# A mixture of experts as one unbroken sequence of steps: the next expert's first up product between the last transposes and the last down product

## What is computed

```python
def moe_swiglu(h, w_router, w1, w3, w2):
    logits = (h @ w_router).astype(jnp.float32)
    top_val, top_idx = lax.top_k(logits, TOP_K)          # TOP_K = 2 of N_EXPERTS = 8
    probs = jax.nn.softmax(top_val, axis=-1)
    combine = jnp.sum(jax.nn.one_hot(top_idx, N_EXPERTS, dtype=jnp.float32) * probs[..., None], axis=-2)
    out = jnp.zeros_like(h)
    for e in range(N_EXPERTS):
        out = out + combine[..., e:e + 1] * swiglu(h, w1[e], w3[e], w2[e])   # (silu(h @ w1) * (h @ w3)) @ w2
    return out
```

## Time and profile before

| | us |
|---|---|
| median of 3 runs | 2117.86 |
| lowest, highest | 2117.47, 2119.53 |
| time of the profiled execution | 2120.26 |
| its span, first to last instruction | 2118.5 |
| busy in the span: PE | 2027.8 |
| DVE | 1609.6 |
| ACT | 1233.7 |

### The profile page before, as it was taken

One profiled execution on the slowest core, in us unless ns is written; L12 is line 12 of the kernel. 1 busy time (PEld: TensorE's weight loads), 2 busy tenths in 40 slices (PEclk: granted clock), 3 DMA queues, 4 the chain that ended last, 5 costly groups with the idle time before them and its releaser, 6 DMA issues.

```text
span 2118.5 us, 28922 instructions
## 1 busy us (share of the span) xinstructions
PE 2027.8 (96%) x10759; PEld 1728.0 (82%) x10759; DVE 1609.6 (76%) x1256; ACT 1233.7 (58%) x1013; POOL 16.5 (1%) x22
## 2 busy tenths in 40 slices
PE   7999999989997999999979999999999999999997
PEld 6998888879997988888868878888887888888885
DVE  5878865755445878955766888898888889888985
ACT  4544455444433554455446777777777777777774
POOL 0000000000000000000000000000000000000000
PEclk9999999999999999999988999999999999999999
DMA  8523455245554522455247999999999999999994
GB/s 279 160 80 100 140 178 179 89 151 188 179 190 136 177 82 90 145 164 186 91 149 260 387 344 378 359 362 368 353 379 341 382 358 364 375 341 372 351 375 179
DMA packets 240481, 516.97 MB, mean 244 GB/s; under 512 B 11519, under 2 KB 34167, under 8 KB 240412
## 3 DMA queue, kind: packets, MB, share of 16 engines
q1 hardware_dynamic: 238124, 507.60, 68.1%
q0 software_dynamic: 2288, 8.41, 1.1%
HBM read 513.86 MB, written 2.12 MB: 244 GB/s over the span
## 4 chain that ended last, share of the span: by engine, by line
PE 87%; DVE 7%; ACT 3%; issue 2%; DMA 0%; SPq 0%; DVEq 0%; ACTq 0%
PE PS L476 25%; PE PS L478 25%; PE PS L477 25%; PE PS L547 7%; DVE lo L1533 2%; ACT hi L1102 2%; PE PS L1002 1%; PE PS L978 1%; PE PS L496 1%; PE PS L758 0%; DVE a_act L1634 0%; DMA rows<-in_knorm_c 0%; PE PS L948 0%; PE PS L789 0%; DVE t_n L1556 0%
## 5 line engine op out<-in xcount | busy, mean ns | idle before, releaser
L1533 DVE TENSOR_TENSOR lo<-raw,hi 128x2048 fp32r<-128x2048 f32 x481 | 1095.0, 2290 | 295.0 <-ACT hi L1102 292.3
L1102 ACT ACTIVATE hi<-raw 128x2048 fp32r<-128x2048 f32 x481 | 919.6, 1915 | 337.8 <-PE PS L478 330.5
L476 PE MATMUL PS<-hi,e_hi 128*128 128x512 f32 x896 | 355.3, 397 | 1.4 <-DVE e_lo L1556 1.4
L478 PE MATMUL PS<-hi,e_lo 128*128 128x512 f32 x896 | 350.2, 391 | 0.0
L477 PE MATMUL PS<-lo,e_hi 128*128 128x512 f32 x896 | 350.2, 391 | 0.0
L476 PE MATMUL PS<-hi,actT_hi 128*128 128x512 f32 x640 | 253.9, 397 | 4.6 <-DVE lo L1533 4.1
L478 PE MATMUL PS<-hi,actT_lo 128*128 128x512 f32 x640 | 249.6, 390 | 0.0
L477 PE MATMUL PS<-lo,actT_hi 128*128 128x512 f32 x640 | 249.1, 389 | 0.0
L476 PE MATMUL PS<-hi,fT_hi 128*128 128x512 f32 x536 | 210.6, 393 | 9.8 <-DVE fT_lo L1556 9.3
L477 PE MATMUL PS<-lo,fT_hi 128*128 128x512 f32 x536 | 209.5, 391 | 0.0
L478 PE MATMUL PS<-hi,fT_lo 128*128 128x512 f32 x536 | 209.3, 390 | 0.0
(11 more groups left out here) (323 smaller groups left out, 2153.8 us busy)
## 6 DMA issues: line engine op xcount, KB each, us to landing
raw<-in_moe_w SPq DMA_DIRECT2D x336, 1024.0 KB, 5.8
raw<-in_w_in SPq DMA_DIRECT2D x92, 1024.0 KB, 5.2
raw<-in_ffn_w SPq DMA_DIRECT2D x33, 1024.0 KB, 5.3
raw<-in_w_br SPq DMA_DIRECT2D x12, 1024.0 KB, 5.0
raw<-in_w_out SPq DMA_DIRECT2D x8, 1024.0 KB, 5.2
hankel<-hankel_dram POOLq DMA_DIRECT2D x1, 1536.0 KB, 13.6
x<-in_x SPq DMA_DIRECT2D x2, 512.0 KB, 4.0
gain<-in_norm_mix POOLq DMA_DIRECT2D x2, 512.0 KB, 5.8
```

What stands on the lines that cost most here:

```text
L476: pe.matmul(out, a_hi, b_hi, start=first, stop=False, skip_group_check=True)
L478: return pe.matmul(out, a_lo, b_hi, start=False, stop=last, skip_group_check=True)
L1102: act.activation(hi[prog.u % SPLIT][:, :], raw[slot][:, :], COPY).then_inc(hi_made.sem, 1)
L1533: dve.tensor_tensor(lo[prog.u % RAW][:, :], raw[prog.u % RAW][:, :], hi[s][:, :].bitcast(F32), ALU.subtract).then_inc(lo_made.sem, 1)
```

## The change

PE's list: the down product of an expert's last step is no longer its end. It comes after the first up product of the next expert, so the eight experts are one sequence of 56 steps. `turn_rows` moves ahead of the last step's up product, and the scatter of the expert before, with the transposes of `pick`, moves between the two halves of the up product of step 1. ACT's and DVE's lists and SyncE's loads follow. Two experts' tokens are now alive at once, so `e_hi` and `e_lo` get a second buffer; `y_hi` and `y_lo` move to where `bias` was. Which buffer an expert uses depends on its number being odd or even, so the loop over six experts becomes one over three pairs, with both experts written out in its body. The inner loop has four turns instead of five, and the last step is written out.

Cut to its core (the parts left out are the second buffer's index and the loops' counters):

```diff
@@ PE: expert @@
+            def step(m, first=False):
+                for w in range(2):
+                    up(w)
+                down(m - 1, first=first)
+                turn_f(m)
+
             pe.wait_ge(e_lo_made.sem, e_lo_made.count(2 * n + 2))
-            up()
+            for w in range(2):
+                up(w)
+            if not first:
+                down(base - 1, last=True)
+            turn_f(base)
+            up(0)
             if not first:
                 scatter(n - 1)
             for t in range(TT):
                 ins = pe.transpose(PS[:, 3, t * P:(t + 1) * P], pick[:, t, :], ident)
             ins.then_inc(pickT_done.sem, 1)
-            turn_f(base)
-            up()
+            up(1)
             if not first:
                 pe.wait_ge(s_read.sem, s_read.count(2 * n - 1))
             down(base, first=True)
...
-            with prog.loop(pe, STEPS_EXPERT - 2, 0) as i:
-                up()
-                down(base + 1 + i)
-                turn_f(base + 2 + i)
+            with prog.loop(pe, STEPS_EXPERT - 3, 0) as i:
+                step(base + 2 + i)
             if not last:
...
-            down(base + STEPS_EXPERT - 1, last=True)
+            step(base + STEPS_EXPERT - 1)
+            if last:
+                down(base + STEPS_EXPERT - 1, last=True)
...
-            with prog.loop(pe, E - 2, 0, rounds=EXPERT_R) as e:
-                expert(E * turn + 1 + e, turn, False, False)
...
+            with prog.loop(pe, PAIRS - 1, 0, rounds=2 * EXPERT_R) as i:
+                for s in (1, 0):
+                    expert(i * 2 + (n + 2 - s), s, turn, False, False)
@@ ACT: expert @@
             prep(1)
-            silu(base, U + 2)
-            prep(2)
+            silu(base, U + 2 if first else U)
+            prep(2 if first else 4)
+            if not first:
+                results(U + 4)
+            high(base)
+            prep(1)
+            prep(1)
+            silu(base + 1, U + 6)
+            prep(1)
             act.wait_ge(pickT_done.sem, pickT_done.count(n + 1))
             act.activation(flat(pickT), PS[:, 3, 0:T], COPY).then_inc(pickT_made.sem, 1)
-            high(base)
+            prep(3)
+            high(base + 1)
             prep(1)
@@ DVE: expert @@
-            prep(2)
-            multiply(base, U + 4)
+            prep(2 if first else 3)
+            multiply(base, U + (4 if first else 2))
+            prep(1 if first else 2)
             if not first:
-                add_to_x(n - 1, e - 1, 0)
+                results(n - 1)
+            low(base)
             prep(1)
-            low(base)
-            prep(2)
+            prep(1)
             if not first:
-                add_to_x(n - 1, e - 1, 1)
-            if not last:
-                choose(n + 1, e + 1, turn)
+                for t in range(TT):
+                    add_to_x(n - 1, e - 1, t)
             prep(2)
             multiply(base + 1, U + 8)
             prep(2)
+            if not last:
+                choose(n + 1, e + 1, turn)
             low(base + 1)
             if not last and turn == 0:
                 keep_row(n + 1)
@@ SyncE: experts @@
+            up(0, 0)
+            with prog.loop(sp, E - 1, 0, rounds=EXPERT_R) as e:
+                steps(e)
+                up(e + 1, 0)
+                down(e, (STEPS_EXPERT - 1) * SUBE)
+            steps(E - 1)
+            down(E - 1, (STEPS_EXPERT - 1) * SUBE)
```

More of the change, by code:

```diff
@@ L67 @@
 EXPERT_R = STEPS_EXPERT
+PAIRS = E // 2
 K_ID, K_LE, K_GT, K_M0, K_MT, K_FLIP, K_N = 0, 1, 2, 3, 4, 11, 12
@@ L264, in build @@
     pickT = sb("pickT", [P, TT, P], F32R)
[L265 to L268, removed]
+    e_hi = [sb(f"e_hi{s}", [P, KT, P], F32R, at=o0 + 8192 * s) for s in range(2)]
+    e_lo = [sb(f"e_lo{s}", [P, KT, P], F32R, at=o0 + 8192 * s + 4096) for s in range(2)]
+    y_hi = sb("y_hi", [P, D], F32R, at=bias_at)
+    y_lo = sb("y_lo", [P, D], F32R, at=bias_at + 4096)
     PS = ctx.enter_context(nc.psum_tensor("PS", [P, 8, 512], F32))
@@ L980, in scatter, with expert, up @@
                 ins.then_inc(s_done.sem, 1)
-        def expert(n, turn, first, last):
+        def expert(n, s, turn, first, last):
             base = STEPS_DENSE + STEPS_EXPERT * n
[L986 to L996, removed]
+            def up(w):
+                for half in range(2):
+                    w_hi, w_lo = unit_ready()
+                    for k in range(4):
+                        a = half * 4 + k
+                        ins = products(PS[:, w, :], e_hi[s][:, a, :], e_lo[s][:, a, :],
+                                       unit_view(w_hi, 4)[:, k, :], unit_view(w_lo, 4)[:, k, :],
+                                       first=a == 0, last=a == KT - 1)
+                    unit_over(ins)
             def turn_f(m):
@@ L1442, in dense, with tokens, results, expert @@
             half_step(m + 1, 0, U + 4 + 3 * m, (0, 0))
-        def tokens(n):
+        def tokens(n, s):
             for j in range(2):
                 act.wait_ge(e_done.sem, e_done.count(2 * n + j + 1))
-                act.activation(e_hi[:, 4 * j:4 * j + 4, :].rearrange("p a b -> p (a b)"), bank(6 + j),
+                act.activation(e_hi[s][:, 4 * j:4 * j + 4, :].rearrange("p a b -> p (a b)"), bank(6 + j),
                                COPY).then_inc(e_hi_made.sem, 1)
-        def expert(n, U, last):
+        def results(used):
+            act.wait_ge(unit_used.sem, used)
+            act.activation(y_hi[:, :], bank(4, 5), COPY).then_inc(y_hi_made.sem, 1)
+        def expert(n, s, U, first, last):
             base = STEPS_DENSE + STEPS_EXPERT * n
@@ L1481, in expert @@
             high(base + m)
-            if not last:
+            if last:
+                results(U + UNITS_EXPERT)
+            else:
                 prep(1)
[L1484 to L1488, removed]
         def experts(turn):
             U = U_END + E * UNITS_EXPERT * turn
[L1492 to L1496, removed]
+            n = E * turn
+            tokens(n, 0)
+            expert(n, 0, U, True, False)
+            with prog.loop(act, PAIRS - 1, 0, rounds=2 * EXPERT_R) as i:
+                for s in (1, 0):
+                    expert(i * 2 + (n + 2 - s), s, i * (2 * UNITS_EXPERT) + (U + (2 - s) * UNITS_EXPERT), False, False)
+            expert(n + E - 1, 1, U + (E - 1) * UNITS_EXPERT, False, True)
         def moe():
@@ L2063, in add_to_x, with results, expert @@
                                      x[:, t, :], ALU.mult, ALU.add).then_inc(s_read.sem, 1)
-        def expert(n, e, turn, U, first, last):
+        def results(n):
+            dve.wait_ge(y_hi_made.sem, n + 1)
+            tt(y_lo[:, :], bank(4, 5), y_hi[:, :].bitcast(F32), ALU.subtract).then_inc(y_lo_made.sem, 1)
+        def expert(n, e, s, turn, U, first, last):
             base = STEPS_DENSE + STEPS_EXPERT * n
@@ L2101, in expert @@
                 prep(1)
+            if not last:
+                tokens(n + 1, 1 - s)
             m = STEPS_EXPERT - 1
@@ L2106, in expert @@
             low(base + m)
-            if not last:
+            if last:
+                results(n)
+            else:
                 prep(1)
[L2109 to L2113, removed]
         def experts(turn):
@@ L2119, in experts @@
             U = U_END + E * UNITS_EXPERT * turn
[L2120 to L2124, removed]
+            tokens(n, 0)
+            expert(n, 0, 0, turn, U, True, False)
+            with prog.loop(dve, PAIRS - 1, 0, rounds=2 * EXPERT_R) as i:
+                for s in (1, 0):
+                    expert(i * 2 + (n + 2 - s), i * 2 + (2 - s), s, turn,
+                           i * (2 * UNITS_EXPERT) + (U + (2 - s) * UNITS_EXPERT), False, False)
+            expert(n + E - 1, E - 1, 1, turn, U + (E - 1) * UNITS_EXPERT, False, True)
             for t in range(TT):
```

57 lines of the change are left out of this document (29 added, 28 removed).

## The result

| | before | after |
|---|---|---|
| median of the timed runs, us | 2118.36 (2116.86 to 2119.53, 14 runs) | 2123.81 (2122.99 to 2125.18, 14 runs) |
| ratio, with its 95% interval | 1 | 1.0026 [1.0019, 1.0033] |
| profiled execution / its span, us | 2120.26 / 2118.5 | 2122.99 / 2121.2 |

The change costs 5.5 us, 0.26%. That lies inside the range (2115.5 to 2124.5), 4.0 us above the number given. It is also just beyond the 0.2% by which "no change" was defined, though the interval, 0.19% to 0.33%, still touches it: taken as it stands the change is slower, which had a chance of 0.20, but none of the three rivals behind that chance (b, c, d) occurred. The two profiled executions are only 2.7 us apart, and the two medians 5.5. That difference is what the later experiments are about.

What follows compares the result with a forecast made beforehand. PE (TensorE), busy 121.63 of 122.80 us per expert, was taken as the bound. The terms -9.8 - 2.0 + 0.8 + 13.0 = +2.0 us gave a median of 2119.8 us, range 2115.5 to 2124.5.

Steps and rivals of the forecast that it cites:

- (b): Rival: DVE's backlog reaches `choose`, so the wait for `pick` grows to 2.35 us and the time to 2123.3; chance 0.08.
- (c): Rival: the longer loop body of two experts makes two jumps back wait for instructions, 2125.6 us; chance 0.07.
- (d): Rival: weights land late, one unit per expert by 0.5 us, +3.5 us, giving 2123.3; chance 0.06.
- -9.8: At seven expert boundaries, PE's wait for `fT_lo` and the restart losses behind it go: -9.8 us.
- -2.0: In step 1 of six experts, a late DVE conversion no longer stretches PE's up and down products: -2.0 us.
- forecast 11.0: Net gain in the expert stage without the new wait, from -9.8, -2.0 and +0.8 added on PE: 11.0 us.
- The new wait, +13.0: After step 1's transposes, the `ids` products wait for DVE's `pick` comparisons, 1.85 us with restart, seven times: +13.0 us.
- The order as a whole: Sum of all terms of the new order, -9.8 - 2.0 + 0.8 + 13.0: +2.0 us.
- the author's own narrower range: Median of 2118 to 2122 us, from the bounds of the new wait and a microsecond for the schedule.

Runs made afterwards that it cites:

- the old order with the late `choose`: Kernel before, with the two comparisons that write `pick` moved behind two conversions on DVE and PE's order kept: 2138.4 us, 1.0093.
- the kernel with the early `choose`: Kernel after, with the two comparisons that write `pick` moved ahead of two conversions on DVE: 2108.68 us, 0.9951.
- 972.76: Kernel after with those comparisons moved ahead of two conversions, plus idle transposes in PE's two last waits: 2106.4 us, 0.9941.
- The kernel after with its waits filled: Kernel after, with 15 idle transposes on PE ahead of each `ids` product, in the wait for `pick`: 2121.27 us, 1.0012.
- before in pairs: Kernel before, with its loop over six experts made one over three pairs, no instruction reordered: 2118.58 us, 1.000.

## Why the prediction was right or wrong

**What goes, -9.8 and -2.0: right.** Of the second, 0.30 us of the 0.34 per expert were seen by themselves, in the old order with the late `choose`. Together, a middle expert of the kernel with the early `choose` gains 1.74 us, forecast 1.66. From the first up product to the last scatter, the two profiles whose only low stretch there is the one at the start (972.76 and 984.40) are 11.6 us apart, forecast 11.0.

**The new wait, +13.0: right.** 1.73 us by the starts on PE (forecast 1.83; PE's reaction was 0.10 shorter than assumed), 1.84 by the periods of two kernels, forecast 1.85. Seven times 1.84 are 12.9.

**The order as a whole: right.** -11.6 + 12.9 = +1.3 us, forecast +2.0. The kernel after with its waits filled and before in pairs differ by 985.75 - 984.40 = 1.35 in this stage, and the profiled executions of after and before, which both have a low stretch at the start and at the end, by 988.66 - 987.35 = 1.31. DVE kept the schedule: the conversion for the down product, the additions and `y_lo` made no one wait; rival (b) fell at that, (c) by the loop over pairs, and (d) because ACT waited for weights only once in the whole stage after, 1.0 us (before: twice, 1.8).

**What was missing: the clock and the end.** The measured time lies outside the author's own narrower range, and inside the wide one only by the room kept there for (b) and (d), which did not come: that part is luck. The step that failed is "Own range of this case: 2118 to 2122, from the bounds of the wait and a microsecond for the schedule." It priced a wait of PE at its length alone. A kernel whose PE was busy 121.63 of 122.80 us ran at full clock, and I took that as given, although the waits of 1.84 and 2.46 us stood in the trace with a low stretch in the first one's wake that I had not looked for. For the profiled pair this adds up: 1.31 in the stage, 0.10 by which the stage starts later, 1.11 in the last scatter and the code behind it, 0.18 after that, together 2.7. The 1.11 is in these rows, which answer to the earlier trace rows. PE's last scatter, kernel after:

```profile
2107.77 0.47 PE L980 MATMUL PS<-y_hi,pickT 128*128 128x512 f32 x1 [2.46 <-DVE y_lo L1583]
...
2108.68 0.63 PE L980 MATMUL PS<-y_lo,pickT 128*128 128x512 f32 x1
2109.11 0.63 PE L980 MATMUL PS<-y_hi,pickT 128*128 128x512 f32 x1
```

DVE's last instruction, kernel after:

```profile
2116.43 0.06 DVE L2231 MEMSET stat<- 128x1 f32 x1 [4.09 <-issue]
```

The clock is low at this scatter too, where before its products start 0.23 us apart, and the skip at the end stands at 4.09 us instead of 3.86.

For the medians, filling the `pick` waits takes back 3.1 of the 5.5 us (5.5 less the 2.4 by which the filled kernel is slower than before), and its profile lacks 2.9 us of low stretches (1.47 in the first expert, 1.62 at the end, less 0.18 in the middle). The filled kernel's 2.4 us are what was forecast for the order, 2.0. So the 5.5 us are the order's exchange plus low clock in the executions of after, which those of before mostly escape. That they escape it is shown by the mean granted clock of the timed executions: 0.989 in 44 of 49 of before, 0.984 to 0.987 in all 23 of after. Where in the timed executions the clock fell is not on record; it is inferred from the few profiled ones.

**Open.** Why six of seven equal waits let the clock fall in the old order with the late `choose`, and none of the middle ones in the kernel after. The waits are equally long and stand behind the same products; what differs in the rows is the expert's period, 125.97 or 122.90 us, and the work in the last step. Also open is why filling the `pick` wait, at most in the middle of the stage, removed the low stretch at its end.

## What to carry to other kernels

When work is moved off an engine's critical path, look at each instruction queued ahead of the producer of what the next consumer needs: here two comparisons, 0.48 us together, cost 13 us in the wrong place, and one place earlier they caused no wait. Price a wait of TensorE with two numbers, its length and what the clock does behind it, and compare more than one profiled execution, and the mean granted clock of the timed ones, before a difference of a few microseconds is put down to the order. Where a wait of TensorE can't be removed, idle transposes in it are cheap and can keep the clock up.

## What the runs showed of the hardware

- A wait of 1.73 us on a TensorE that is busy 99% of the time let its clock fall to 1.2 GHz in some places and not in others; where it fell, it cost 1.58 us more. Fifteen idle transposes in each wait took away 8.7 us.
- At 2.4 GHz the products of 512 columns start 0.23 us apart, and 0.43 at 1.2 GHz.
- The mean granted clock told fast from slow executions of one kernel: all five executions of before at 0.987 were slower than all 44 at 0.989.
- A loop body of over 1000 instructions on TensorE repeated without a stall, with one packet on each of two instruction queues in 500 us.
- Products started 0.05 us after the comparisons of `pick` ended on DVE (1398.60 + 0.48 to 1399.13), against the 0.15 and 0.24 us seen before.
